# The dt columns of a Mamba projection moved from place 16 to place 2 and computed token-major, and the first half of three layer norms normalised one step earlier

## The chip, the cores and the metric

The kernel runs on one NeuronCore of a Trainium2 chip, as a single program. The metric is the device time of one execution in microseconds (us); lower is better. The core's engines are TensorE (PE in the profile; PEld are its weight loads), VectorE (DVE), ScalarE (ACT), GpSimd (POOL) and the queue that issues most loads (SP). Each runs its own instruction list in order and waits for the others on semaphores.

## The reference

Two transformer blocks run one after the other on 256 tokens of width 1024, in float32. The first block has two layers: attention and an MLP, then a bidirectional Mamba-2 mixer and an MLP, each sublayer followed by a layer norm. The second block (two layers of SwiGLU, convolution with differential attention, SwiGLU) is not touched by the change. What the change touches is this:

```python
def layer_norm(x, g, b):
    xf = x.astype(jnp.float32)
    mu = jnp.mean(xf, -1, keepdims=True)
    var = jnp.mean(jnp.square(xf - mu), -1, keepdims=True)
    return ((xf - mu) * lax.rsqrt(var + LN_EPS)).astype(x.dtype) * g + b

def mamba2_bidir_mixer(x, w_in, conv_w, conv_b, dt_bias, a_log, ...):
    zxbcdt = x @ w_in                      # 256 x 1024 times 1024 x 6208
    z, xbc, dt = jnp.split(zxbcdt, [SSM_D_INNER, SSM_D_INNER + SSM_CONV_DIM], axis=-1)
    xbc = jax.nn.silu(depthwise_conv_centred(xbc, conv_w, conv_b))
    xs, bm, cm = jnp.split(xbc, ...)       # 2048, 1024, 1024 columns
    dt = jax.nn.softplus((dt + dt_bias).astype(jnp.float32))    # 64 columns
    a_neg = -jnp.exp(a_log.astype(jnp.float32))
    # both directions: cumulative sums of dt * a_neg per head, their exponentials,
    # and products with bm, cm and xs in chunks of 128 tokens
    ...
    y = (y_f + y_b) + xs * d_skip[:, None]
    y = y * jax.nn.silu(z)                 # then a grouped RMS norm and the output product
```

## The kernel before

**Weights in units.** Every product with weights is cut into units: 1024 rows by 256 columns of a weight matrix, 1 MB, one after the other through three slots (`RING`). SP loads unit u into `w_raw` once the low part of unit u - 3 is made. ACT rounds it to `w_hi` (`split`, L735; it waits until PE is done with unit u - 3), and DVE or, for units 2 to 16 of the Mamba projection and some later ones, POOL computes the remainder `w_lo` = `w_raw` - `w_hi` (L1132, L646). PE then takes three products of high and low parts, all issued from one line (`three`, L1692). `unit_done` counts the units that PE has finished. In the names of the trace `pg<-op_hi,w_hi` is a product written to the PSUM buffer `pg` in which the activations stream and the weights are stationary; `pg<-w_hi,op_hi` is the other way round.

**Two orientations.** `feature_chunk` (L1699) puts 128 weight columns into the array and streams 256 tokens, so features come out on the partitions. `token_tile` (L1708) puts 128 tokens into the array and streams the weight columns, so tokens come out on the partitions. Both take 8 pieces of the inner dimension by 3 products, 24 matmuls for one result tile. A full unit has two tiles, 48 matmuls.

**The Mamba projection.** It has 25 units in the order of `SSM_COLS`: 16 that go through the convolution (n = 0 to 15: 8 for B and C, 8 for xs), one with the 64 dt columns (n = 16, `DT_AT`), and 8 for z (n = 17 to 24). For a convolution unit DVE does ten operations (L1452, L1456) and ACT a SiLU (`conv_act`, L932) one unit later; the eight xs units are also turned to token-major by PE (L1998) and copied out by DVE (`xs_evac`). The dt unit is one `feature_chunk` of 24 matmuls, after which the 64 dt features lie on 64 partitions (`dt_v`). DVE adds the bias (L1417), ACT computes the parts of softplus (L959 to L962, with an exponential of `a_col` between), DVE joins them two units later (L1420), computes the cumulative sums and the pair `g_pair` (L1425 to L1433), PE turns dt to token-major (L1989) and DVE copies that into `dt_tok` (L1436). All of this is needed only in the stage that follows the projection (chunked scan, from about 505 us).

**The layer norms.** The last unit before a layer norm is ordered so that its four sums of 128 tokens by 512 columns end one after the other (`output` with `last`, L1727). DVE (`ln`, L1175) takes each: it adds the residual (L1183) and takes statistics (L1186); after the second and the fourth sum it combines them for token tile 0 and tile 1 (L1189). ACT computes the standard deviation (L768), DVE its reciprocal (L1173) and the normalised tile `xn` (L1207, one instruction for tile 0, four for tile 1). PE turns `xn` to feature-major (L1757), 8 transposes of tile 0 and 8 of tile 1, in that order; ACT scales each pair of tile 1's (L757), DVE splits it (L1149, L1150), and the next projection begins. In norms 1, 2 and 3 the normalisation of tile 0 stands behind the statistics of the fourth sum; in norm 4, which goes another way, it stands behind the third.

Of the kernel before, what the change touches and what calls it, by code (L numbers as in the profile page):

```python
# [14 lines left out]
P = 128  # L15
# [40 lines left out]
CONV_UNITS = 2 * Z_UNITS  # L56
# [3 lines left out]
XS_AT = 10  # L60
# [136 lines left out]
def two_blocks(nc, A, out):  # L197
    with ExitStack() as ctx:
# [103 lines left out]
        dt_bias = cv(1)  # L302
# [6 lines left out]
        dt_v, dt_a = h32[0:64, 0:T], h32[0:64, T:2 * T]  # L309
# [293 lines left out]
        def _(pool):  # L603
# [68 lines left out]
            pool.dma_start(dt_bias[0:64, :], A["ssm_dt_bias"].rearrange("a (d o) -> (a d) o", o=1)).then_inc(small_in, 16)  # L672
# [9 lines left out]
            pool.wait_ge(g_ready, 1)  # L682
            pool.wait_ge(dtT_done, 1)
# [48 lines left out]
        def _(act):  # L732
# [215 lines left out]

            for n in range(len(SSM_COLS)):
# [3 lines left out]
                if 1 <= n <= CONV_UNITS:  # L953
                    conv_act(n - 1)
                if n > DT_AT:
                    if n == DT_AT + 1:

                        act.wait_ge(dt_sum, 1)
                        link(act.activation(dt_a, dt_v, ACT.Abs))  # L959
                        link(act.activation(dt_a, dt_a, ACT.Exp, scale=-1.0))  # L960
                        act.activation(a_col[0:64, :], a_col[0:64, :], ACT.Exp).then_inc(dt_soft, 1)
                        act.activation(dt_a, dt_a, ACT.Ln, bias=1.0).then_inc(dt_soft, 1)  # L962
                    z = n - DT_AT - 1
                    act.wait_ge(unit_done, u + 1)
                    act.activation(silz[:, :, z * U:z * U + U], pair, ACT.Silu).then_inc(z_ready, 1)
# [155 lines left out]
        def _(dve):  # L1121
# [53 lines left out]
            def ln(u_last, k, apply):  # L1175
# [235 lines left out]
            dve.memset(one_col, 1.0)  # L1411
            for n in range(len(SSM_COLS)):
                split(U_SSM + n + 2)
                if n == DT_AT:
                    dve.wait_ge(unit_done, U_SSM + n + 1)
                    dve.wait_ge(small_in, 64)
                    dve.tensor_scalar(dt_v, pg[0:64, n % 4, 0:T], dt_bias[0:64, :], None, ALU.add).then_inc(dt_sum, 1)  # L1417
                if n == DT_AT + 2:
                    dve.wait_ge(dt_soft, 2)
                    dve.scalar_tensor_tensor(out=dt_v, in0=dt_v, scalar=0.0, in1=dt_a, op0=ALU.max,  # L1420
                                             op1=ALU.add).then_inc(dt_ready, 1)
                if n == DT_AT + 3:

                    dve.wait_ge(dt_ready, 1)
                    link(dve.tensor_scalar(aT[0:64, :], dt_v, a_col[0:64, :], -1.0, ALU.mult, ALU.mult))  # L1425
# [11 lines left out]
                if n < CONV_UNITS:  # L1437
                    i = n
# [22 lines left out]
                if XS_AT <= n < XS_AT + Z_UNITS:  # L1461
                    xs_evac(dve, n - XS_AT)
# [220 lines left out]
        def _(pe):  # L1683
# [285 lines left out]

            for n in range(len(SSM_COLS)):  # L1970
                u = U_SSM + n
                bank = pg[:, n % 4, :]
                if n >= 4:
                    m = n - 4
                    if m < CONV_UNITS:
                        pe.wait_ge(conv_done, m + 1)
                    elif m == DT_AT:
                        pe.wait_ge(dt_sum, 1)
                    else:
                        pe.wait_ge(z_ready, m - DT_AT)  # L1980
# [5 lines left out]
                if n == DT_AT + 3:  # L1986
# [4 lines left out]
                if XS_AT <= n < XS_AT + Z_UNITS:  # L1991
                    j = n - XS_AT
# [201 lines left out]
```

## Time and profile before

| what | value |
|---|---|
| median of 3 runs | 1882.2 us (1876.39 to 1884.85) |
| the profiled execution's own time | 1882.2 us |
| its span in the trace | 1880.3 us |
| mean granted TensorE clock | 0.979 of full speed |
| busy share of the span, PE | 96% |
| DVE, ACT, POOL | 57%, 46%, 15% |
| the chain that ended last: PE, DVE, ACT, issue | 87%, 8%, 3%, 1% |
| projection of the Mamba mixer | 357.9 to 504.9 us |
| layer norms 1, 2, 3 | from about 156, 348 and 625 us |

The span runs from the first to the last instruction of the trace; the execution's own time is 1.9 us longer. Busy shares are averages over very different stages, so each stage is read by itself. PE's matmuls are pipelined: a record lasts about 0.28 us while the next one starts 0.12 us later, so the distance between starts is what a matmul costs, not the length of its record.

### The profile page before, as it was taken

To read this page: it belongs to the slowest core of one execution; us is meant where nothing else is said; L and a number is where in the kernel's file an instruction comes from. 1 tells how busy PE (TensorE), PEld (TensorE's weight loads), DVE (VectorE), ACT (ScalarE), POOL (GpSimd) and SP (SyncE) were. 2 spreads that over 40 slices of the span, in tenths; PEclk is the share of its full clock that TensorE was granted. 3 is DMA by queue.
4 is the path that set the end of the run, shared out by engine and by line. 5 is a ranking of instruction groups with operands and counts; after the bars stand their busy time and mean duration, and the time that the engine had idled before them with its cause. 6 is when DMAs were issued, how large, how long until landed. Compare 5 with 4: busy or idle time off the path is not lost.

```text
span 1880.3 us, 29790 instructions
## 1 busy us (share of the span) xinstructions
PE 1806.5 (96%) x12217; PEld 1655.4 (88%) x12217; DVE 1072.9 (57%) x1438; ACT 863.9 (46%) x1137; POOL 286.1 (15%) x155
## 2 busy tenths in 40 slices
PE   8988999999999899989999998999999999989999
PEld 7757999899997799979998977999899989779998
DVE  5567555668576755564544574454554445745444
ACT  4354444445555344454335646434543446464342
POOL 2003000286241300000000730000000006300000
PEclk9899999999999999989999999999999999989999
DMA  9303655564502465535554521655455554316552
GB/s 298 113 1 129 210 193 184 151 189 143 200 1 89 145 225 190 190 123 187 182 182 153 174 96 59 208 180 184 151 201 180 185 171 158 112 45 202 179 185 105
DMA packets 211135, 293.99 MB, mean 156 GB/s; under 512 B 6426, under 2 KB 184064, under 8 KB 211056
## 3 DMA queue, kind: packets, MB, share of 16 engines
q1 hardware_dynamic: 207936, 285.62, 45.5%
q0 software_dynamic: 2688, 6.47, 1.4%
q8 instruction: 56, 0.92, 0.2%
q10 hardware_dynamic: 432, 0.79, 0.1%
q14 instruction: 23, 0.19, 0.0%
HBM read 291.81 MB, written 1.05 MB: 156 GB/s over the span
## 4 chain that ended last, share of the span: by engine, by line
PE 87%; DVE 8%; ACT 3%; issue 1%; DMA 0%; POOL 0%; SPq 0%; ACTq 0%; DVEq 0%
PE pg L1692 52%; PE acc L1692 26%; PE acc L2037 1%; DVE acc L1566 1%; PE pg L2133 1%; PE pg L1757 1%; PE acc L1958 1%; DVE w_lo L1132 1%; PE pg L1756 1%; PE pg L2021 1%; PE pg L2023 1%; DVE stats L1186 1%; PE pg L1934 1%; DVE X L1183 1%; DVE arena L1627 1%
## 5 line engine op out<-in xcount | busy, mean ns | idle before, releaser
L1132 DVE TENSOR_TENSOR w_lo<-w_raw,w_hi 128x2048 fp32r<-128x2048 f32 x231 | 539.1, 2336 | 393.6 <-ACT w_hi L742 393.5
L1692 PE MATMUL pg<-op_hi,w_hi 128*128 128x256 f32 x2544 | 725.6, 285 | 5.0 <-DVE op_lo L1150 3.1
L1692 PE MATMUL pg<-op_lo,w_hi 128*128 128x256 f32 x2544 | 720.4, 283 | 0.0
L1692 PE MATMUL pg<-op_hi,w_lo 128*128 128x256 f32 x2544 | 720.4, 283 | 0.0
L742 ACT CAST w_hi<-w_raw 128x2048 fp32r<-128x2048 f32 x270 | 514.4, 1905 | 219.3 <-PE pg L1692 141.2
L1692 PEld LDWEIGHTS pg<-op_hi,w_hi 128*128 128x128 f32 x2544 | 488.4, 192 | 13.4 <-issue 7.6
L1692 PEld LDWEIGHTS pg<-op_hi,w_lo 128*128 128x128 f32 x2544 | 488.6, 192 | 3.3 <-issue 0.5
L1692 PEld LDWEIGHTS pg<-op_lo,w_hi 128*128 128x128 f32 x2544 | 488.5, 192 | 0.0
L1692 PE MATMUL acc<-w_hi,op_hi 128*128 128x512 f32 x768 | 303.7, 395 | 5.6 <-DVE op_lo L1256 4.4
L1692 PE MATMUL acc<-w_lo,op_hi 128*128 128x512 f32 x768 | 302.1, 393 | 0.0
L1692 PE MATMUL acc<-w_hi,op_lo 128*128 128x512 f32 x768 | 301.0, 392 | 0.0
L646 POOL TENSOR_TENSOR w_lo<-w_raw,w_hi 128x2048 fp32r<-128x2048 f32 x39 | 179.7, 4611 | 572.1 <-DVE w_lo L1132 435.9
L1692 PEld LDWEIGHTS acc<-w_hi,op_hi 128*128 128x128 f32 x768 | 146.1, 190 | 35.5 <-issue 5.5
L1692 PEld LDWEIGHTS acc<-w_hi,op_lo 128*128 128x128 f32 x768 | 145.7, 190 | 31.3
L1692 PEld LDWEIGHTS acc<-w_lo,op_hi 128*128 128x128 f32 x768 | 146.3, 190 | 27.6
L802 ACT CAST op_hi<-h 128x512 fp32r<-128x512 f32 x76 | 47.1, 620 | 259.4 <-PE acc L1692 213.5
L795 ACT ACTIVATE act_buf<-pg 128x512 f32<-128x512 f32 x76 | 45.4, 597 | 236.6 <-PE pg L1692 236.6
L1256 DVE TENSOR_TENSOR op_lo<-h,op_hi 128x512 fp32r<-128x512 f32 x76 | 55.4, 729 | 113.5 <-ACT op_hi L802 113.5
L1566 DVE SCALAR_TENSOR_TENSOR acc<-arena,pcol,acc 128x256 f32<-128x256 f32 x174 | 71.1, 481 | 0.6
L1692 PE MATMUL pg<-w_hi,op_hi 128*128 128x256 f32 (+1 forms) x240 | 68.6, 286 | 0.0
L1692 PE MATMUL pg<-w_lo,op_hi 128*128 128x256 f32 (+1 forms) x240 | 67.7, 282 | 0.0
L1692 PE MATMUL pg<-w_hi,op_lo 128*128 128x256 f32 (+1 forms) x240 | 67.7, 282 | 0.0
(269 smaller groups left out, 1542.4 us busy)
## 6 DMA issues: line engine op xcount, KB each, us to landing
w_raw<-in_mlp_w SPq DMA_DIRECT2D x64, 1024.0 KB, 5.3
w_raw<-in_ffn_w_gate SPq DMA_DIRECT2D x44, 1024.0 KB, 5.1
w_raw<-in_ffn_w_up SPq DMA_DIRECT2D x44, 1024.0 KB, 5.1
w_raw<-in_ffn_w_down SPq DMA_DIRECT2D x44, 1024.0 KB, 4.8
w_raw<-in_ssm_w_in SPq DMA_DIRECT2D x24, 1024.0 KB, 5.4
w_raw<-in_w_in SPq DMA_DIRECT2D x20, 1024.0 KB, 5.0
w_raw<-in_attn_w_in SPq DMA_DIRECT2D x9, 1024.0 KB, 9.4
w_raw<-in_ssm_w_out SPq DMA_DIRECT2D x8, 1024.0 KB, 4.8
```

The costliest lines, as they stand in the source:

```text
L646: pool.tensor_tensor(w_lo[:, r, :], w_raw[:, r, :], w_hi[:, r, :].bitcast(F32), ALU.subtract) \
L742: act.copy(w_hi[:, u % RING, :], w_raw[:, u % RING, :]).then_inc(hi_ready, 1)
L795: act.activation(act_buf[:, :], src, func).then_inc(act_done, 1)
L802: act.copy(op_hi[:, at_chunk:at_chunk + 2, :], h32[:, :].rearrange("p (c t) -> p c t", c=2)).then_inc(h_hi, 1)
L1132: dve.tensor_tensor(w_lo[:, s, :], w_raw[:, s, :], w_hi[:, s, :].bitcast(F32), ALU.subtract) \
L1183: dve.scalar_tensor_tensor(out=x, in0=x, scalar=ALPHA, in1=acc[:, q, :], op0=ALU.mult, op1=ALU.add).then_inc(x_new, 1)
L1186: ins = dve.bn_stats(stats[:, t, a, :], x)
L1256: dve.tensor_tensor(op_lo[:, dst, :], h32[:, :].rearrange("p (c t) -> p c t", c=2), op_hi[:, dst, :].bitcast(F32), ALU.subtract).then_inc( ...
L1566: ins = dve.scalar_tensor_tensor(out=conv_bank(c) if k < CK - 1 else cacc[:, c, :], in0=uu[:, c, k:k + T], scalar=w, in1=conv_bank(c), op0 ...
L1627: dve.tensor_scalar(n2[:, s, :], m2[:, s, :], -1.0, None, ALU.mult).then_inc(mx2_ready, 1)
L1692: ins = pe.matmul(psum, l, r, start=first and i == 0, stop=last and i == 2)
L1756: return pe.matmul(o, X[:, t, j * P:(j + 1) * P], diag[:, t, :], start=True, stop=True)
```

## The change

It has two parts, which don't depend on each other.

1. The dt unit moves from n = 16 to n = 2, and the rest keep their order: convolution units at n = 0, 1 and 3 to 16, z units at n = 17 to 24. It is computed with `token_tile`, two tiles of 24 matmuls with 64 streamed columns each, in place of one `feature_chunk` with 256 streamed tokens. Tokens lie on the partitions, so the bias is loaded as a row for all 128 partitions, the softplus runs on 128 x 128 elements in place of 64 x 256 and writes `dt_tok` directly, and PE turns `dt_tok` to feature-major for the cumulative sums. On ACT the exponential of `a_col` stands behind the logarithm. DVE waits for the softplus right after it has added the bias, in front of the convolution of n = 3.
2. In norms 1 to 3 tile 0 is normalised after the third sum, before the fourth is added.

```diff
-SSM_COLS = [2 * DI + i * U for i in range(8)] + [DI + i * U for i in range(Z_UNITS)] + [2 * DI + 2 * SG * SN] \
-    + [i * U for i in range(Z_UNITS)]
-DT_AT = CONV_UNITS
+SSM_COLS = [2 * DI + i * U for i in range(2)] + [2 * DI + 2 * SG * SN] + [2 * DI + i * U for i in range(2, 8)] \
+    + [DI + i * U for i in range(Z_UNITS)] + [i * U for i in range(Z_UNITS)]
+DT_AT = 2
...
         # ACT, the projection's loop
+                if n == DT_AT:
+                    act.wait_ge(dt_sum, 1)
+                    link(act.activation(dt_a, dt_v, ACT.Abs))
+                    link(act.activation(dt_a, dt_a, ACT.Exp, scale=-1.0))
+                    act.activation(dt_a, dt_a, ACT.Ln, bias=1.0).then_inc(dt_soft, 1)
+                    act.activation(a_col[0:64, :], a_col[0:64, :], ACT.Exp).then_inc(dt_soft, 1)
+                    continue
...
         # DVE, ln()
-                    if q == 2 and k == 4:
+                    if q == 2:
                         apply(k, 0)
                 if k == 4:
                     rms(5, 0)
-                else:
-                    apply(k, 0)
                 apply(k, 1)
...
         # DVE, the projection's loop
                 if n == DT_AT:
                     dve.wait_ge(unit_done, U_SSM + n + 1)
                     dve.wait_ge(small_in, 64)
-                    dve.tensor_scalar(dt_v, pg[0:64, n % 4, 0:T], dt_bias[0:64, :], None, ALU.add).then_inc(dt_sum, 1)
+                    dve.tensor_tensor(dt_v, pg[:, n % 4, 0:128].rearrange("p (t n) -> p t n", t=TT),
+                                      dt_bias.unsqueeze(1).broadcast_to([P, TT, 64]), ALU.add).then_inc(dt_sum, 1)
+                    dve.wait_ge(dt_soft, 2)
+                    dve.scalar_tensor_tensor(out=dt_tok, in0=dt_v, scalar=0.0, in1=dt_a, op0=ALU.max,
+                                             op1=ALU.add).then_inc(dt_ready, 1)
+                    continue
                 if n == DT_AT + 2:
+                    dve.wait_ge(dtT_done, 1)
+                    link(dve.tensor_scalar(aT[0:64, :], acc[0:64, 0, 0:T], a_col[0:64, :], -1.0, ALU.mult, ALU.mult))
...
-                if n == DT_AT + 4:
-                    dve.wait_ge(dtT_done, 1)
-                    link(dve.tensor_copy(dt_tok, acc[:, 0, 0:P].rearrange("p (t n) -> p t n", t=TT)))
...
         # PE, the projection's loop
                 if n == DT_AT:
                     take(u)
-                    feature_chunk(u, bank[:, 0:T], 0, step=64).then_inc(unit_done, 1)
-                else:
-                    project(u, bank, tokens=n > DT_AT, fresh="ln2_0" if n == 0 else None)
-                if n == DT_AT + 3:
+                    for t in range(TT):
+                        ins = token_tile(u, bank[:, t * 64:t * 64 + 64], t, 0, 64, step=64)
+                    ins.then_inc(unit_done, 1)
+                    continue
+                project(u, bank, tokens=n >= 17, fresh="ln2_0" if n == 0 else None)
+                if n == DT_AT + 1:
                     pe.wait_ge(dt_ready, 1)
                     for t in range(TT):
-                        ins = pe.transpose(acc[:, 0, t * 64:t * 64 + 64], dt_v[:, t * P:t * P + P], ident[0:64, 0:64])
+                        ins = pe.transpose(acc[0:64, 0, t * P:t * P + P], dt_tok[:, t, :], ident[:, :])
                     ins.then_inc(dtT_done, 1)
```

The counts in the semaphore waits, the loops' indices and the turning of the xs units follow the new order.

ACT around the dt unit before, where it stands between the convolution units and z (`h` is the buffer of `dt_v` and `dt_a`; `arena` here is `a_col`, the sums of the convolution or z):

```order
L742 CAST w_hi<-w_raw 128x2048 [waits unit_done,raw_ready1]
L959 ACTIVATE h<-h 64x256 [waits dt_sum]
L960 ACT_TABLE_LOAD
L960 ACTIVATE h<-h 64x256 [waits act_link]
L961 ACTIVATE arena<-arena 64x1 [waits act_link]
L962 ACT_TABLE_LOAD
L962 ACTIVATE h<-h 64x256
L965 ACT_TABLE_LOAD
L965 ACTIVATE arena<-pg 128x2x256 [waits unit_done]
```

And now, behind the split of unit 4 (the row with `unit_done,raw_ready1`):

```order
L739 CAST w_hi<-w_raw 128x2048 [waits unit_done,raw_ready1]
L953 ACTIVATE h<-h 128x128 [waits dt_sum]
L954 ACT_TABLE_LOAD
L954 ACTIVATE h<-h 128x128 [waits act_link]
L955 ACT_TABLE_LOAD
L955 ACTIVATE h<-h 128x128 [waits act_link]
L956 ACT_TABLE_LOAD
L956 ACTIVATE arena<-arena 64x1
L739 CAST w_hi<-w_raw 128x2048 [waits unit_done,raw_ready2]
L942 ACT_TABLE_LOAD
L942 ACTIVATE arena<-arena,pcol 128x256 [waits conv_done]
```

The softplus now stands between the splits of units 4 and 5, with a table load of its own for each of Exp, Ln, Exp and the SiLU that follows, and the splits of all later units stand behind it.

DVE in the second layer norm before, from the third sum on:

```order
L1183 SCALAR_TENSOR_TENSOR X<-X,acc 128x512
L1186 BN_STATS stats<-X 128x6
L1183 SCALAR_TENSOR_TENSOR X<-X,acc 128x512
L1186 BN_STATS stats<-X 128x6
L1189 BN_AGGR mv<-stats 128x2
L1173 RECIPROCAL rstd<-std 128x1
L1207 TENSOR_SCALAR xn<-X,mv,rstd 128x1024
L1173 RECIPROCAL rstd<-std 128x1
L1207 TENSOR_SCALAR xn<-X,mv,rstd 128x256 x4
```

And now:

```order
L1187 SCALAR_TENSOR_TENSOR X<-X,acc 128x512
L1190 BN_STATS stats<-X 128x6
L1177 RECIPROCAL rstd<-std 128x1
L1209 TENSOR_SCALAR xn<-X,mv,rstd 128x1024
L1187 SCALAR_TENSOR_TENSOR X<-X,acc 128x512
L1190 BN_STATS stats<-X 128x6
L1193 BN_AGGR mv<-stats 128x2
L1177 RECIPROCAL rstd<-std 128x1
L1209 TENSOR_SCALAR xn<-X,mv,rstd 128x256 x4
```

The reciprocal and the normalisation of tile 0 moved ahead of the fourth sum; between the combination of tile 1's statistics (BN_AGGR) and the reciprocal that needs ACT's answer to it, nothing is left.

DVE at the dt unit now (`arena<-h` writes `dt_tok`; the rows before and behind are convolutions):

```order
L1456 SCALAR_TENSOR_TENSOR arena<-pg,pcol,arena 128x254 [waits dve_link] x2
L1420 TENSOR_TENSOR h<-pg,arena 128x128 [waits small_in,unit_done]
L1423 SCALAR_TENSOR_TENSOR arena<-h 128x128 [waits dt_soft]
L1452 TENSOR_SCALAR arena<-pg,pcol 128x256 [waits conv_silu,unit_done]
L1452 TENSOR_SCALAR arena<-pg,pcol 128x256
L1456 SCALAR_TENSOR_TENSOR arena<-pg,pcol,arena 128x254 [waits dve_link] x2
```

The add and the joining of the softplus stand next to each other, ahead of the convolution of n = 3; in the kernel before, two splits and two copies stood between them.

## Rows read from the trace of the kernel before

**Rows 1.** The page's fourth part: the chain that ended last, by engine.

```profile
PE 87%; DVE 8%; ACT 3%; issue 1%; DMA 0%; POOL 0%; SPq 0%; ACTq 0%; DVEq 0%
```

**Rows 2.** DVE by time, second layer norm: start us, us, engine, line, operation.

```profile
353.06 0.21 DVE L1189 BATCH_NORM_AGGREGATE mv<-stats 128x2 f32<-128x12 f32 x1
353.18 0.11 DVE L1173 RECIPROCAL rstd<-std 128x1 f32<-128x1 f32 x1
353.33 0.81 DVE L1207 TENSOR_SCALAR xn<-X,mv,rstd 128x1024 f32<-128x1024 f32 x1
354.06 0.15 DVE L1173 RECIPROCAL rstd<-std 128x1 f32<-128x1 f32 x1
354.25 1.38 DVE L1207 TENSOR_SCALAR xn<-X,mv,rstd 128x256 f32<-128x256 f32 x4
```

**Rows 3.** ACT by time, second norm; in brackets idle us before, and the releaser.

```profile
353.30 0.29 ACT L768 ACTIVATE std<-mv,lnb 128x1 f32<-128x1 f32 x1 [2.48 <-DVE mv L1189]
...
355.55 1.93 ACT L757 ACTIVATE turn_buf<-pg,pcol 128x256 f32<-128x256 f32 x4 [1.16 <-PE pg L1757]
```

**Rows 4.** PE by time, second norm: the 16 transposes.

```profile
354.20 1.97 PE L1757 MATMUL pg<-ident,xn 128*128 128x128 f32 x16 [2.77 <-DVE xn L1207]
```

**Rows 5.** ACT, then DVE, by time, fourth norm: a reciprocal released by ACT.

```profile
831.70 0.29 ACT L789 ACTIVATE std<-ssum,part 128x1 f32<-128x1 f32 x1
...
832.03 0.16 DVE L1173 RECIPROCAL rstd<-std 128x1 f32<-128x1 f32 x1 [1.53 <-ACT std L789]
```

**Rows 6.** PE, then ACT, by time, third norm.

```profile
631.98 3.45 PE L1757 MATMUL pg<-ident,xn 128*128 128x128 f32 x16 [2.78 <-DVE xn L1207]
...
634.19 1.93 ACT L757 ACTIVATE turn_buf<-pg,pcol 128x256 f32<-128x256 f32 x4 [2.81 <-PE pg L1757]
```

**Rows 7.** A stretch; the last columns are granted clock, DMA share, GB/s.

```profile
632.00:636.00 4.00, 4.00 (x19) 3.52 (x20) 2.10 (x6) 1.81 (x4) 2.90 (x5) 0.57 0.54 153
```

**Rows 8.** PE by time, dt unit: first and last of 24 matmuls.

```profile
454.48 0.36 PE L1692 MATMUL pg<-op_hi,w_hi 128*128 128x256 f32 x1
...
457.30 0.28 PE L1692 MATMUL pg<-op_lo,w_hi 128*128 128x256 f32 x1
```

**Rows 9.** PE by time, first and last of 48 matmuls with 128 streamed columns.

```profile
26.88 0.22 PE L1692 MATMUL pg<-w_hi,op_hi 128*128 128x128 f32 x1
...
32.07 0.28 PE L1692 MATMUL pg<-w_hi,op_lo 128*128 128x128 f32 x1
```

**Rows 10.** PE by time, scan stage: 8 matmuls with 64 streamed columns.

```profile
523.56 1.00 PE L2037 MATMUL acc<-arena 128*128 128x64 f32 x8
```

**Rows 11.** DVE, then ACT, by time, the dt unit's sum and softplus.

```profile
463.66 0.47 DVE L1417 TENSOR_SCALAR h<-pg,arena 64x256 f32<-64x256 f32 x1
...
464.16 0.42 ACT L959 ACTIVATE h<-h 64x256 f32<-64x256 f32 x1 [2.33 <-DVE h L1417]
464.60 1.28 ACT L960 ACT_TABLE_LOAD   x1
...
466.34 0.20 ACT L961 ACTIVATE arena<-arena 64x1 f32<-64x1 f32 x1
```

**Rows 12.** ACT, POOL, DVE by time, units 1 to 4 of the projection.

```profile
371.64 1.91 ACT L742 CAST w_hi<-w_raw 128x2048 fp32r<-128x2048 f32 x1 [0.75 <-PE pg L1692]
...
373.63 4.63 POOL L646 TENSOR_TENSOR w_lo<-w_raw,w_hi 128x2048 fp32r<-128x2048 f32 x1 [0.94 <-ACT w_hi L742]
...
371.58 0.88 DVE L1452 TENSOR_SCALAR arena<-pg,pcol 128x256 f32<-128x256 f32 x2 [1.64 <-PE pg L1692]
...
377.34 0.88 DVE L1452 TENSOR_SCALAR arena<-pg,pcol 128x256 f32<-128x256 f32 x2 [1.63 <-PE pg L1692]
```

**Rows 13.** DVE, then ACT, by time, units 17 to 20 of the projection.

```profile
459.61 4.13 DVE L1132 TENSOR_TENSOR w_lo<-w_raw,w_hi 128x2048 fp32r<-128x2048 f32 x1
...
475.74 0.60 ACT L965 ACTIVATE arena<-pg 128x512 f32<-128x512 f32 x1 [1.47 <-PE pg L1692]
...
481.94 0.60 ACT L965 ACTIVATE arena<-pg 128x512 f32<-128x512 f32 x1 [3.81 <-PE pg L1692]
```

More of the change, by code:

```diff
@@ L301, in two_blocks @@
         ssm_c = prow[:, :, :].rearrange("p a n -> p (a n)")[:, 0:384]
-        dt_bias = cv(1)
+        dt_bias = cv(64)
         d_skip = cv(SH)
@@ L308, in two_blocks @@
         aT, gT = act_buf[:, 0:T], act_buf[:, T:2 * T]
-        dt_v, dt_a = h32[0:64, 0:T], h32[0:64, T:2 * T]
+        dt_v, dt_a = (h32[:, i * P:i * P + P].rearrange("p (t n) -> p t n", t=TT) for i in range(2))
         xD = [b[:, :].rearrange("p (t n) -> p t n", t=TT) for b in (act_buf, h32)]
@@ L671, in _ @@
             pool.wait_ge(h_ready, HG_MLP[0] + G1)
-            pool.dma_start(dt_bias[0:64, :], A["ssm_dt_bias"].rearrange("a (d o) -> (a d) o", o=1)).then_inc(small_in, 16)
+            pool.dma_start(dt_bias, A["ssm_dt_bias"].broadcast_to([P, 64])).then_inc(small_in, 16)
             pool.dma_start(d_skip, A["ssm_D"].broadcast_to([P, SH])).then_inc(small_in, 16)
@@ L680, in _ @@
             rows_load(2)
-            pool.wait_ge(g_ready, 1)
-            pool.wait_ge(dtT_done, 1)
+            pool.wait_ge(dt_ready, 1)
             pool.wait_ge(small_in, 64)
@@ L947, in conv_act @@
                 ins.then_inc(conv_silu, 1)
+            i = 0
             for n in range(len(SSM_COLS)):
@@ L951, in _ @@
                 split(u + 2)
-                pair = pg[:, n % 4, :].rearrange("p (c t) -> p c t", c=2)
[L953 to L963, printed above, removed]
+                if n == DT_AT:
[5 more added lines that the diff above has]
+                    continue
+                pair = pg[:, n % 4, :].rearrange("p (c t) -> p c t", c=2)
+                if n < len(SSM_COLS) - Z_UNITS:
+                    if i >= 1:
+                        conv_act(i - 1)
+                    i += 1
+                else:
+                    if i == 16:
+                        conv_act(15)
+                        i += 1
+                    z = n - (len(SSM_COLS) - Z_UNITS)
                     act.wait_ge(unit_done, u + 1)
@@ L1411, in _ @@
             dve.memset(one_col, 1.0)
+            i = 0
             for n in range(len(SSM_COLS)):
@@ L1460, in _ @@
                     ins.then_inc(conv_done, 1)
-                if XS_AT <= n < XS_AT + Z_UNITS:
-                    xs_evac(dve, n - XS_AT)
+                    i += 1
+                    if i >= 11:
+                        xs_evac(dve, i - 11)
+                elif i == 16:
+                    xs_evac(dve, 6)
+                    xs_evac(dve, 7)
+                    i += 1
             dve.wait_ge(const_in, CONST_SSM)
@@ L1967, in _ @@
             turn("ln2_0", xn)
+            i = 0
             for n in range(len(SSM_COLS)):
@@ L1974, in _ @@
                     m = n - 4
-                    if m < CONV_UNITS:
+                    if m < DT_AT:
                         pe.wait_ge(conv_done, m + 1)
@@ L1978, in _ @@
                         pe.wait_ge(dt_sum, 1)
+                    elif m < 17:
+                        pe.wait_ge(conv_done, m)
                     else:
-                        pe.wait_ge(z_ready, m - DT_AT)
+                        pe.wait_ge(z_ready, m - 16)
                 if n == DT_AT:
                     take(u)
-                    feature_chunk(u, bank[:, 0:T], 0, step=64).then_inc(unit_done, 1)
-                else:
-                    project(u, bank, tokens=n > DT_AT, fresh="ln2_0" if n == 0 else None)
-                if n == DT_AT + 3:
+                    for t in range(TT):
[4 more added lines that the diff above has]
+                if n == DT_AT + 1:
                     pe.wait_ge(dt_ready, 1)
                     for t in range(TT):
-                        ins = pe.transpose(acc[:, 0, t * 64:t * 64 + 64], dt_v[:, t * P:t * P + P], ident[0:64, 0:64])
+                        ins = pe.transpose(acc[0:64, 0, t * P:t * P + P], dt_tok[:, t, :], ident[:, :])
                     ins.then_inc(dtT_done, 1)
-                if XS_AT <= n < XS_AT + Z_UNITS:
-                    j = n - XS_AT
+                if n >= 11 and n < 19:
+                    j = n - 11
                     pe.wait_ge(conv_silu, j + 9)
```

10 lines of the change are left out of this document (1 added, 9 removed).

## The prediction

> **What bounds the kernel now.** I read the chain that ended last first, then PE's waits, then the engines by time in the two stretches that the change touches. The chain is 87% PE [rows 1], so what changes PE's matmul time or makes PE wait changes the total, and what DVE, ACT and POOL do beside it is free as long as it is early enough. In the projection PE starts a unit every 5.76 us, the distance between two units' convolutions [rows 12], and is never idle. In a layer norm the roles turn: PE stands, and DVE works without a gap from the first sum to the last normalised quarter, so there DVE sets the end [rows 2]. PE waits 2.77 us for tile 0 and then runs all 16 transposes back to back [rows 4].
>
> **The dt unit on PE.** Before: 24 matmuls from 454.48 to 457.30 plus one step, 24 x 0.12 = 2.9 us [rows 8]. After: 48 matmuls, each with a full load of 128 token columns and only 64 streamed columns. The trace has no fp32r matmul of this width. The nearest from above is the same kind with 128 streamed columns: (32.07 - 26.88) / 47 = 0.110 us from start to start [rows 9], hardly less than the 0.12 of 256 columns, so below 256 columns the streamed width no longer sets the pace. The nearest from below is a plain float32 matmul with 64: eight in 1.00 us, of which the last one's tail is about 0.28, so (1.00 - 0.28) / 7 = 0.103 [rows 10]. That gives 4.9 to 5.3 us; I take 5.3, from the row of the same type. Term: 5.3 - 2.9 = +2.4 us, all on PE's path (bounds +2.0 and +2.4 when pipelined; the third rival has them not pipelined).
>
> A rule speaks for less. The Trainium skill, "TensorE: Matmul & The Clock Gate", section "Back-to-back issue gap", puts 1 to 64 streamed columns at about 25 ns, or 62 ns with the sequencer's decoding. By 62 ns the unit would take 3.0 us and the whole come to 1882.8 us (the sixth rival); but the same page says of real streams that the weight load counts too, and the rows with 64 and 128 columns, 0.103 and 0.110, side with that.
>
> **The softplus at its new place.** I work in the clock of the trace before. Unit 1 ends at 371.58, since DVE starts its convolution there [rows 12]. The dt unit, now unit 2, ends 5.3 later, at 376.9; unit 3 at 376.9 + 5.76 = 382.7. From DVE's add to ACT's first operation it took 464.16 - 463.66 = 0.50 with 256 elements; with 128 I take 0.4, so ACT starts at 377.3. Then Abs, load, Exp, load, Ln, load, Exp of `a_col`. A load is 1.28; an operation on 256 elements 0.42, on one 0.20 [rows 11], so on 128 about 0.3; with 0.03 between them it is 3 x 0.3 + 0.2 + 3 x 1.28 + 0.2 = 5.1 us. ACT is done at 382.4.
> - Queued behind it on DVE is the joining (0.3) and the convolution of n = 3, whose data comes at 382.7: nothing lost. PE waits for `dt_ready` after unit 3, so from 382.7 for at most 0.1.
> - Queued behind it on ACT is the split of unit 5, which was free to start at 376.9. It runs 382.4 to 384.3 (1.91), POOL follows 0.08 later and takes 4.63 [rows 12]: the low part of unit 5 is there at 384.4 + 4.6 = 389.0. PE ends unit 4 at 382.7 + 5.76 and the two transposes of dt, worth (481.94 - 475.74) - 5.76 = 0.44 [rows 13]: 388.9. So PE waits 0.1, and the stall of `dt_ready` is part of it.
> - Then ACT also loads the SiLU table and does one convolution before the split of unit 6 (382.4 + 1.9 + 1.3 + 0.9 + 1.9 = 388.4); POOL takes it up at 389.0 and ends at 393.6, PE wants it at 394.7. POOL needs 4.63 of each 5.76, so the slack comes back by 1.1 us per unit.
>
> Term: +0.2 us. Bounds: 0, if the operations take as on one element; +0.8, if they take as long as with 256 (0.4 more) and POOL is slowed a little by DVE's cumulative sums, which now run beside its splits. The 0.44 of the transposes was paid before as well. The three ACT operations, one load less, the copy into `dt_tok` and the sums that leave the z units free nothing: PE was never idle from unit 17 to the end of the projection. The new bias load on POOL's queue is issued where the old one was, ahead of the second norm. SP's loads keep their order otherwise; a dt unit early is a short load early, and slot 2 is then waited for as before.
>
> **The three layer norms.** DVE does the same work in another order. Reciprocal and normalisation of tile 0 take 354.06 - 353.18 = 0.88 and move ahead of the fourth sum. So tile 0's transposes (8 x 0.11) run while DVE works on the fourth sum and are out of the way. But the combination for tile 1 comes 0.88 later, at 353.94 in the second norm, and ACT's answer is no longer hidden behind tile 0: ACT began 0.24 after the combination's start and took 0.29 [rows 3], and a reciprocal that ACT releases starts 0.04 after it ends [rows 5]: 353.94 + 0.57 = 354.51. The normalisation of tile 1 follows 0.19 later, at 354.70, not at 354.25 [rows 2]. Its first quarter (0.40 long) is there at 355.10 and PE can begin tile 1 at 355.16. Before, PE began tile 1 after eight transposes, at 354.20 + 0.88 = 355.08 [rows 4]. The first pair, which ACT waited for (355.55, [rows 3]), is thus 0.1 us later, and everything behind it in the same rhythm. Term: 3 x 0.1 = +0.3 us. Bounds for one norm: -0.88, if tile 0's transposes were all that counted, and +0.45, if tile 1's delay counted in full.
>
> **The sum.** 2.4 + 0.2 + 0.3 = +2.9 us on the profiled execution's own 1882.2 us (span 1880.3 and 1.9 around it), which equals the median: 1885.1 us, +0.15%. I call "same" what is within 0.5% (9.4 us), about what a measurement of this kernel can tell; the three runs of before alone span 8.5 us.
>
> **The rivals.**
> - Second: the layer norms give. In the third norm the granted clock was 0.57 over 632 to 636 [rows 7], 1.2 and not 2.4 GHz for most of it: the 16 transposes took 3.45 us and not 1.97, and ACT's first pair came 2.21 us after PE's start in place of 1.35 [rows 6], 0.86 later. With tile 0's transposes done beforehand only two stand before that pair, so most of 0.86 comes back if the clock falls again; if PE's shorter idle times keep the clock up, that and some matmul time in the second norm come back too. All three norms at -0.88 and 0.9 more make -3.5; with +2.6 for the projection: 1881.3 us. Against it is the count above, in which DVE's chain and not the transposes ends last.
> - Third, slower: the small matmuls don't overlap. If each cost its record of 0.275 us, the dt unit would take 13.2 us, +10.3, and with the rest +10.8: 1893.0 us. It becomes slower by over 0.5% from 0.24 us per matmul on. Both small-width rows, in which starts are 0.10 to 0.11 apart, speak against it.
> - Fourth, slower in part: ACT's chain is twice as dear. Then the low part of unit 5 and all behind it is late. With the four operations and three loads as in the rows there is 0.1 us of lateness, so every further us on ACT goes straight to PE. One us for each of three loads would make +2.9 more: 1888.0 us. The rows show Exp starting right as the load ends (464.60 + 1.28, and 466.34 after two operations of 0.42), so I see no hidden us.
> - Fifth: a late stall. DVE now works on xs copy 7 after unit 18 and only then on the low part of unit 20. POOL's work on X lies there, beside which a DVE split took 4.13 [rows 13]. From the end of unit 18 and its transposes the copy takes 0.7 and the split 4.1, PE wants it after unit 19's 5.76: 1 us to spare. If both are slowed further, some 1 us more: 1886 us.
> - Sixth: the width counts after all below 128 columns, and a matmul with 64 costs about half of 0.110. Then the dt unit takes 2.6 to 3.0 us, its term is 0, and the whole is 1882.8 us. The scan's 0.103 with the same width [rows 10] is against it, though those matmuls are plain float32.
>
> On the fourth, the Trainium skill, "ScalarE: Activation LUTs", section "What ACT_TABLE_LOAD costs", adds a drain of about 1.38 us to each load's 1.28. By that the three loads ahead of the split of unit 5 would cost 4.1 us more, and all of it would be stall: 1889.2 us. The rows show no such gap between operation, load and operation.
>
> **How the numbers follow.** Chances: first 0.59, second 0.15, third 0.04, fourth 0.10, fifth 0.04, sixth 0.05; 0.03 for what I don't see. Half-speed spells of the clock elsewhere shift with every change of phase and can move any of these by 2 or 3 us. The first case's own range is 1882 to 1888; with the second and the fourth it is 1879 to 1890. Slower by over 0.5% takes the third or a fourth at over three times its estimate: 0.05. Faster by over 0.5% would need more than all that the norms can give: 0.03.
>
> **What would show it.** Right: the 48 small matmuls 0.10 to 0.11 us apart; three table loads between DVE's add and the split of unit 5, and a PE wait below 0.5 us at unit 5; in each norm PE's transposes in two groups with idle time between them, DVE idle about 0.5 us before the reciprocal of tile 1, and the first pair at ACT within 0.2 us of before, counted from the first sum. Wrong: a PE gap of over 1 us in units 4 to 6 or 19 to 21; small matmuls over 0.2 us apart; a first pair at ACT 0.5 us earlier in a norm at full clock.

## The result and the profile after

The changed kernel takes 1890.7 us (median of 6 runs, 1886.4 to 1892.4), the kernel before 1881.6 us in its own 6 (1875.9 to 1884.9): 9.0 us more, a ratio of 1.0052 with a 95% interval of 1.0032 to 1.0073. I had predicted 1885.1 us with a range of 1879 to 1890. The sign and the size of the dt unit were right; the whole came out three times as dear as forecast, and just outside the range.

The profiled execution took 1886.6 us. This is the first line of its page, and the chain that ended last by engine:

```profile
span 1884.5 us, 29836 instructions
...
PE 85%; DVE 10%; ACT 3%; issue 1%; DMA 0%; POOL 0%; SPq 0%; ACTq 0%; DVEq 0%
```

The span is 4.2 us longer than before (1880.3). That is less than the 9.0 us of the medians, and for a reason that has nothing to do with the change. In the attention stage, which is the same in both kernels, the clock fell to 1.2 GHz for a different length in the two profiled executions. The stretch 90 to 100 us before (busy us and, in brackets, instructions of PE, its weight loads, DVE, ACT and POOL, then the granted clock, the DMA share and GB/s):

```profile
90.00:100.00 10.00, 10.00 (x25) 5.27 (x24) 4.38 (x14) 3.60 (x14) 0.00 (x0) 0.51 0.00 0
```

And after:

```profile
90.00:100.00 10.00, 9.30 (x41) 5.33 (x40) 6.67 (x22) 4.88 (x18) 0.00 (x0) 1.00 0.01 2
```

The first sum of norm 1 came at 155.56 us before and at 150.35 after: 5.2 us that belong to no edit. In the profiled executions of the ten experiments below it came at 150 to 152 us in eight and at 155 in two (5 and 10), so both moments are seen with the old and with the new order of units. I therefore compare stages. From the first sum of norm 2 to the scan's first output (DVE) it is 172.9 us before and 183.6 after, +10.7; all other stages together, without the 5.2, make -1.3. The projection itself, from its first to its last matmul, went from 146.8 to 157.3 us. Three things fill these 10.5 us (they add up to 10.4).

**The dt unit on PE, +2.4.** Two of its matmuls:

```profile
365.37 0.28 PE L1697 MATMUL pg<-w_hi,op_lo 128*128 128x64 f32 x1
365.48 0.28 PE L1697 MATMUL pg<-w_hi,op_hi 128*128 128x64 f32 x1
```

They start 0.11 apart, as the row with 128 columns [rows 9] had said: 48 of these against 24 at 0.12 [rows 8].

**A PE wait for a low part, +3.3.** I had allowed 0.1 at unit 5; it came at unit 8, and large. PE:

```profile
402.51 0.28 PE L1697 MATMUL pg<-op_lo,w_hi 128*128 128x256 f32 x1
406.08 0.36 PE L1697 MATMUL pg<-op_hi,w_hi 128*128 128x256 f32 x1 [3.29 <-POOL w_lo L644]
```

It goes back to DVE. DVE from the convolution of n = 3 (L1456) on; L1429 to L1437 are the cumulative sums and `g_pair`, which the change put behind it and ahead of the convolution of n = 4:

```profile
380.38 3.33 DVE L1456 SCALAR_TENSOR_TENSOR arena<-pg,pcol,arena 128x254 f32<-128x254 f32 x8
383.62 0.47 DVE L1429 TENSOR_SCALAR act_buf<-acc,arena 64x256 f32<-64x256 f32 x1
384.12 4.23 DVE L1430 TENSOR_TENSOR_SCAN act_buf<-arena,act_buf 64x256 f32<-64x256 f32 x1
388.39 4.66 DVE L1431 TENSOR_TENSOR act_buf<-act_buf 32x256 f32<-32x256 f32 x1
393.08 0.42 DVE L1433 CAST g_pair<-act_buf 64x512 fp32r<-64x512 f32 x1
...
394.44 0.88 DVE L1452 TENSOR_SCALAR arena<-pg,pcol 128x256 f32<-128x256 f32 x2
```

POOL beside it (low parts of units 5 to 7 back to back, then of 8 and 9), and ACT:

```profile
378.59 14.18 POOL L644 TENSOR_TENSOR w_lo<-w_raw,w_hi 128x2048 fp32r<-128x2048 f32 x3 [6.60 <-ACT w_hi L739]
401.38 9.13 POOL L644 TENSOR_TENSOR w_lo<-w_raw,w_hi 128x2048 fp32r<-128x2048 f32 x2 [8.61 <-ACT w_hi L739]
...
371.65 0.31 ACT L953 ACTIVATE h<-h 128x128 f32<-128x128 f32 x1 [4.27 <-DVE h L1420]
...
376.63 1.89 ACT L739 CAST w_hi<-w_raw 128x2048 fp32r<-128x2048 f32 x1
...
398.60 0.91 ACT L942 ACTIVATE arena<-arena,pcol 128x256 f32<-128x256 f32 x2 [11.09 <-DVE arena L1456]
399.41 1.89 ACT L739 CAST w_hi<-w_raw 128x2048 fp32r<-128x2048 f32 x1
```

The first of POOL's three operations ends at 383.2, the second at 387.8 and the third at 392.8. The scan begins at 384.12 and ends at 388.35, 0.5 us after POOL's second; the next operation begins at 388.39 and ends at 393.05, 0.3 after POOL's third. Once POOL pauses, the rest take 0.42 each. POOL gave way too, but by little: its third operation, which started just before the scan got through, took 5.00 us in place of 4.63. The same two operations in the kernel before, at a place where POOL was idle (472.8 to 480.4):

```profile
477.78 0.68 DVE L1426 TENSOR_TENSOR_SCAN act_buf<-arena,act_buf 64x256 f32<-64x256 f32 x1
478.50 0.42 DVE L1427 TENSOR_TENSOR act_buf<-act_buf 32x256 f32<-32x256 f32 x1
```

So the chain of six took 10.8 us (383.62 to 394.41) instead of 2.9 (477.40 to 480.28), and the next convolution came late, ACT waited 11.09 us for it with the split of unit 8 queued behind it (399.41), POOL got that at 401.38, and PE ran dry at 402.5.

**The clock, +4.7.** At half speed the starts of matmuls are 0.21 apart instead of 0.12. Counting the steps of the projection between 0.19 and 0.23 us gives 25 before and 75 after (some ten in each have another reason, such as the turning of the xs units); at 0.094 each that is 2.4 and 7.1 us. Stretches of the changed kernel: the dt unit, its second half, and the time behind the wait:

```profile
365.00:370.00 5.00, 5.00 (x47) 5.00 (x46) 4.08 (x10) 1.90 (x1) 3.94 (x2) 0.99 0.79 250
370.00:376.00 6.00, 6.00 (x30) 6.00 (x30) 0.29 (x1) 4.27 (x6) 2.00 (x1) 0.50 0.64 201
406.00:412.00 6.00, 5.92 (x37) 5.95 (x38) 4.59 (x12) 3.61 (x5) 6.00 (x2) 0.72 0.62 185
```

In the second the clock is at 1.2 GHz nearly throughout, though PE had been issuing a matmul each 0.11 us since 365.26 without a pause. The rows where it changes:

```profile
369.72 0.28 PE L1697 MATMUL pg<-w_hi,op_lo 128*128 128x64 f32 x1
369.83 0.39 PE L1697 MATMUL pg<-w_hi,op_hi 128*128 128x64 f32 x1
370.03 0.40 PE L1697 MATMUL pg<-w_lo,op_hi 128*128 128x64 f32 x1
```

The last of the three stretches has a fall right behind the wait of 3.3 us. Before, the clock was 1.00 over 365 to 380 and 398 to 412; the only spell of its projection was at the first unit, and the changed kernel has that one too, 1.2 us longer within the projection (0.5 us of the 4.7).

**The norms, next to nothing together.** DVE, ACT and PE in the second norm, in the order of time on each:

```profile
341.02 0.69 DVE L1187 SCALAR_TENSOR_TENSOR X<-X,acc 128x512 f32<-128x512 f32 x1 [0.79 <-PE acc L1697]
...
348.12 0.16 DVE L1177 RECIPROCAL rstd<-std 128x1 f32<-128x1 f32 x1 [0.36 <-ACT std L765]
...
349.27 1.93 ACT L754 ACTIVATE turn_buf<-pg,pcol 128x256 f32<-128x256 f32 x4 [0.40 <-PE pg L1762]
...
346.25 1.10 PE L1762 MATMUL pg<-ident,xn 128*128 128x128 f32 x8 [1.25 <-DVE xn L1209]
348.79 1.76 PE L1762 MATMUL pg<-ident,xn 128*128 128x128 f32 x8 [1.45 <-DVE xn L1209]
```

From the first sum to the first pair at ACT it is 349.27 - 341.02 = 8.25 us; before, 355.55 [rows 3] less 347.45 is 8.10. The transposes stand in two groups, DVE idles 0.36 before tile 1's reciprocal. In the first norm the same distance is 8.50 and was 8.14, in the third 8.29 (rows below) and was 8.95 (634.19 [rows 6] less 625.24).

```profile
629.30 0.69 DVE L1187 SCALAR_TENSOR_TENSOR X<-X,acc 128x512 f32<-128x512 f32 x1 [2.59 <-PE acc L1697]
...
637.59 1.93 ACT L754 ACTIVATE turn_buf<-pg,pcol 128x256 f32<-128x256 f32 x4 [1.22 <-PE pg L1762]
```

The stretch 632 to 640 us of the changed kernel:

```profile
632.00:640.00 8.00, 4.69 (x27) 2.85 (x25) 6.77 (x17) 2.63 (x7) 2.73 (x5) 1.00 0.32 29
```

The third norm gives 0.66 us: before, the clock was at 1.2 GHz while all 16 transposes ran [rows 7]; now it is full. That is +0.36, +0.15 and -0.66.

### The profile page after: what moved, and what is told of

Read it like the earlier page. It is cut to its first block, busy times and chain, and to the rows that moved or that the text cites. A ratio compares the mean times of both kernels' runs of the same rounds, so it can differ in the third digit from the quotient of the medians.

```text
span 1884.5 us, 29836 instructions
## 1 busy us (share of the span) xinstructions
PE 1807.6 (96%) x12241; PEld 1658.7 (88%) x12241; DVE 1082.0 (57%) x1437; ACT 864.0 (46%) x1138; POOL 286.6 (15%) x155
## 4 chain that ended last, share of the span: by engine, by line
PE 85%; DVE 10%; ACT 3%; issue 1%; DMA 0%; POOL 0%; SPq 0%; ACTq 0%; DVEq 0%
PE pg L1697 51%; PE acc L1697 25%; PE acc L2047 1%; DVE acc L1571 1%; PE pg L2143 1%; DVE w_lo L1136 1%; ACT w_hi L739 1%; PE pg L2031 1%; PE pg L2033 1%; DVE stats L1190 1%; DVE X L1187 1%; DVE arena L1632 1%; PE pg L1761 1%; PE pg L1762 0%; PE acc L1963 0%
## 5 line engine op out<-in xcount | busy, mean ns | idle before, releaser
L1697 PE MATMUL pg<-w_hi,op_hi 128*128 128x256 f32 (+2 forms) x256 | 73.2, 286 | 0.0
L1697 PE MATMUL pg<-w_lo,op_hi 128*128 128x256 f32 (+2 forms) x256 | 72.5, 283 | 0.0
L1697 PE MATMUL pg<-w_hi,op_lo 128*128 128x256 f32 (+2 forms) x256 | 72.5, 283 | 0.0
```

What stands on the lines that cost most here:

```text
L1697: ins = pe.matmul(psum, l, r, start=first and i == 0, stop=last and i == 2)
```

## The experiments

All were timed in 5 rounds against the kernel before on the same chip. "Stage" below is the time from the first sum of norm 2 to the scan's first output in the profiled execution: 172.9 before, 183.6 in the changed kernel. The theory was: POOL's long operations hold DVE's sums, which makes the wait; the clock falls with the narrow matmuls and behind the wait; the norms are worth nothing. Rivals: the norms cost it; the softplus on ACT costs it; the width of the matmuls alone costs it.

**1. The norms alone** (kernel before with this part of the change):

```diff
-                    if q == 2 and k == 4:
+                    if q == 2:
...
-                else:
-                    apply(k, 0)
```

> The kernel before with the second part of the change alone: tile 0 normalised after the third sum in norms 1 to 3; the dt unit stays at n = 16. If the norms are worth what the prediction says (+0.1 us each), the ratio is 1.000 (+0.3 us) and the first pair reaches ACT within 0.2 us of before, counted from the first sum. If the norms carry a good part of the +9 us, it is 1.002 or more. If they give something back (the second rival), 0.998.

Measured: 1881.5 us against 1880.8, ratio 0.9995 (0.9981 to 1.0009), stage 173.2. In its trace the first pair comes 0.36 and 0.14 us later in norms 1 and 2 and 0.43 earlier in norm 3. Together the reordered norms neither gain nor lose, and the prediction's second rival, 3.5 us back, is out, though its term for the third norm is there in part.

**2. The dt unit alone** (the changed kernel with the edit of experiment 1 undone).

> The changed kernel with the norms as they were before, so the move of the dt unit alone. Theory: the whole loss is in the projection, which went from 146.8 to 157.3 us in the two traces; expected +8 to +11 us on before (ratio 1.005), a PE wait of about 3 us for POOL's low part, and 1.2 GHz for several us from within the dt unit on. Rival: the norms share in it, then +5 or less.

Measured: 1891.7 us, ratio 1.0060 (1.0041 to 1.0078), stage 183.8. All of the loss is here. PE's wait for POOL was 4.27 us this time. On DVE it was another pair of operations that was held, since POOL's operations ended at other times:

```profile
382.51 0.91 DVE L1432 TENSOR_TENSOR_SCAN act_buf<-arena,act_buf 64x256 f32<-64x256 f32 x1
383.46 4.67 DVE L1433 TENSOR_TENSOR act_buf<-act_buf 32x256 f32<-32x256 f32 x1
388.17 4.72 DVE L1435 CAST g_pair<-act_buf 64x512 fp32r<-64x512 f32 x1
```

The scan escaped with 0.91; the operation behind it and the cast took a whole POOL operation each.

**3. The sums late** (changed kernel; the sums back where POOL makes no low parts, and POOL's next work waits for their end):

```diff
-                if n == DT_AT + 2:
+                if n == DT_AT + 17:
...
+            pool.wait_ge(g_ready, 1)
```

> The changed kernel with the cumulative sums of dt (six DVE operations) moved from n = 4 to n = 19, where POOL has no splits any more; PE turns dt at n = 3 as before. Theory: in the change DVE's sums wait for POOL's splits to end (one took 4.23 us and not 0.68, the next 4.66 and not 0.42), the convolution of unit 4, ACT's split and POOL's come late in turn, and PE waits 3.3 us. With the sums late that wait is gone, and the 1.2 GHz that came 2 us behind it: 4 to 5 us faster than the change, +4 to +5 us on before. Rival: ACT's softplus chain makes the wait, since the split of unit 5 stands behind it; then PE's wait of over 1 us stays, and the gain is under 1.5 us.

Measured: 1884.0 us, ratio 1.0018 (1.0001 to 1.0035), stage 177.6. PE waits for POOL no more, though softplus, table loads and narrow matmuls stay: 6.0 of the stage's 10.7 us, or two thirds of the loss by the ratios, were due to the sums' place. DVE's sums there:

```profile
481.63 0.68 DVE L1431 TENSOR_TENSOR_SCAN act_buf<-arena,act_buf 64x256 f32<-64x256 f32 x1
482.35 0.41 DVE L1432 TENSOR_TENSOR act_buf<-act_buf 32x256 f32<-32x256 f32 x1
```

The clock still falls, now just behind the dt unit (its last matmul starts at 374.96, the next unit at 375.07, and the fall comes at 375.2); the stretch 372 to 380 us:

```profile
372.00:380.00 8.00, 8.00 (x57) 8.00 (x57) 2.37 (x7) 4.32 (x6) 4.54 (x1) 0.79 0.69 205
```

**4. 256 columns in the dt unit** (changed kernel; 192 of each 256 columns are computed for nothing):

```diff
-                        ins = token_tile(u, bank[:, t * 64:t * 64 + 64], t, 0, 64, step=64)
+                        ins = token_tile(u, bank[:, t * U:t * U + U], t, 0, U, step=64)
```

> The changed kernel with 256 in place of 64 streamed columns in the 48 matmuls of the dt unit; 192 of them are computed for nothing and not read. By the spacing alone it is slower than the change: 48 x (0.120 - 0.111) = +0.4 us. Theory: the clock fell to 1.2 GHz because the array was streamed only half as densely in that unit (6.8 us at 1.2 GHz from 4.6 us into it, worth 3.2 us); then with full width the clock stays at 2.4 GHz there and it is 2 to 3 us faster than the change. Rival: the fall of the clock is an accident of phase; then +0.4 us, and it shows 1.2 GHz in that place too, or the change loses it in other runs.

Measured: 1888.5 us, ratio 1.0046 (1.0030 to 1.0063), stage 182.0. Over the dt unit, and around the end of the wait of 4.93 us:

```profile
365.00:380.00 15.00, 14.94 (x126) 14.73 (x125) 8.16 (x21) 10.73 (x12) 8.44 (x3) 1.00 0.60 189
405.00:409.00 4.00, 3.75 (x20) 3.78 (x21) 3.96 (x11) 2.71 (x3) 4.00 (x2) 0.59 0.67 197
```

The matmuls are 0.119 apart instead of 0.111, 0.4 us more for the unit, and the clock stays up. Against the changed kernel it is 1.1 us less by the two ratios, which their intervals don't tell from nothing, and 1.6 by the stage, where 2 to 3 had been expected: what the clock gives back goes in part into the wait, 4.93 us in place of 3.29. (The expectation's "half as densely" is no figure of the rows: they show 64 columns in place of 256 at nearly the same spacing.)

**5. POOL's low parts in four pieces** (changed kernel):

```diff
-                pool.tensor_tensor(w_lo[:, r, :], w_raw[:, r, :], ...).then_inc(lo_ready, 1)
+                for q in range(4):
+                    c = slice(q * 512, q * 512 + 512)
+                    ins = pool.tensor_tensor(w_lo[:, r, c], w_raw[:, r, c], ...)
+                ins.then_inc(lo_ready, 1)
```

> The changed kernel with each of POOL's splits issued as four operations on 512 columns in place of one on 2048, for the first and the second block alike; nothing else moves. Theory: a DVE operation with two SBUF operands waits until the POOL operation that is under way has ended, so its longest delay falls from 4.7 to about 1.2 us each; DVE's cumulative sums then take 5 us or less in place of 10.8, the convolution behind them is in time, PE's wait of 3.3 to 4.9 us at this place is gone, and the kernel is 4 to 6 us faster than the change (+3 to +5 on before). Rival: what DVE waits for is the stretch in which POOL is busy at all, three splits in a row; then cutting changes nothing and the wait stays.

Measured: 1870.9 us, ratio 0.9940 (0.9921 to 0.9960), stage 177.7. The same sums at the same place beside POOL, and POOL:

```profile
388.62 1.23 DVE L1432 TENSOR_TENSOR_SCAN act_buf<-arena,act_buf 64x256 f32<-64x256 f32 x1
389.88 1.34 DVE L1433 TENSOR_TENSOR act_buf<-act_buf 32x256 f32<-32x256 f32 x1
391.26 1.40 DVE L1435 CAST g_pair<-act_buf 64x512 fp32r<-64x512 f32 x1
...
384.25 16.19 POOL L646 TENSOR_TENSOR w_lo<-w_raw,w_hi 128x512 fp32r<-128x512 f32 x12 [5.82 <-ACT w_hi L741]
```

POOL's piece is 16.19 / 12 = 1.35 us on average, and every one of DVE's operations now takes 1.2 to 1.4: they pass one per piece. This is what separates the theory from "POOL slows DVE in proportion": the total of work beside them is the same, only the grain changed. Pieces beside DVE's operations took 1.47 us and more, the others 1.3, so POOL gives way here too. PE's wait fell to 0.4 us. The gain went past what I expected (I had looked at the projection only). Two stages of the second block, which the change doesn't touch, became 3.4 and 6.5 us shorter (134.7 to 131.3, 136.3 to 129.8). PE's waits for DVE there (us in total, times, longest us), first before, then in this experiment:

```profile
PE pg L2124 <- DVE arena L1643: 8.6, 4, 3.8
```

```profile
PE pg L2136 <- DVE arena L1650: 2.8, 4, 0.9
```

**6. The kernel before with POOL's work on X in pieces** (256 columns instead of 1024, both products and sums):

```diff
-                    link(pool.tensor_tensor(X[:, t, :], xn[:, t, :], gain_row[:, :], ALU.mult))
+                    for q in range(4):
+                        c = slice(q * 256, q * 256 + 256)
+                        ins = pool.tensor_tensor(X[:, t, c], xn[:, t, c], gain_row[:, c], ALU.mult)
+                    link(ins)
```

> The kernel before with POOL's work on X behind norms 1 to 3 (gain and bias, four operations on 1024 columns per norm) issued as sixteen on 256 columns. Theory: in the trace of before DVE's first square in the MLP behind norm 1 took 2.88 us and not 0.69, and its low part 2.08; both ended as POOL's operations did, PE waited 2.65 us and its clock fell for some us after. With pieces of about 1.1 us these delays shrink to under 1 us each, in norm 3 (a PE wait of 1.74) as well: 3 to 7 us faster than before. Rival: POOL and DVE take turns word by word, then the whole work of POOL costs DVE the same in pieces: no change.

Measured: 1870.7 us, ratio 0.9935 (0.9917 to 0.9953). So the kernel before had the same trouble elsewhere. Behind norm 1, DVE, then POOL, then PE before:

```profile
175.81 2.88 DVE L1260 TENSOR_TENSOR h<-act_buf 128x512 f32<-128x512 f32 x1
179.38 2.08 DVE L1256 TENSOR_TENSOR op_lo<-h,op_hi 128x512 fp32r<-128x512 f32 x1 [0.68 <-ACT op_hi L802]
...
169.43 8.71 POOL L661 TENSOR_TENSOR X<-xn,gain_row 128x1024 f32<-128x1024 f32 x2 [144.18 <-DVE op_lo L1150]
...
181.60 0.71 PE L1692 MATMUL acc<-w_hi,op_hi 128*128 128x512 f32 x1 [2.65 <-DVE op_lo L1256]
```

And here:

```profile
170.22 1.22 DVE L1265 TENSOR_TENSOR h<-act_buf 128x512 f32<-128x512 f32 x1
172.13 1.17 DVE L1261 TENSOR_TENSOR op_lo<-h,op_hi 128x512 fp32r<-128x512 f32 x1 [0.69 <-ACT op_hi L807]
```

The first of them had waited for the end of POOL's second operation (169.43 + 8.71 = 178.14) and ended 0.55 behind it; now it waits for one piece (1.22 us in place of 2.88). PE's wait of 2.65 is gone, norm 1 to norm 2 went from 191.9 to 187.4 us and norm 3 to norm 4 from 193.0 to 189.0. The 10.1 us by the medians are more than the 3 to 7 expected; these two stages give 8.5 of them.

**7. Experiments 3 and 4 together.**

> The changed kernel with both cures: the cumulative sums at n = 19 and 256 streamed columns in the dt unit (192 computed for nothing). Theory: no PE wait for POOL and no fall of the clock within the dt unit; what is left is 48 x 0.12 - 24 x 0.12 = +2.8 us on before. Rival: the clock's fall there is not due to the narrow matmuls; then it comes in this kernel too, and the time is +4 or more.

Measured: 1880.7 us, ratio 1.0003 (0.9989 to 1.0017), stage 176.4; the clock is full from 365 us on and PE doesn't wait for POOL. The interval reaches to +3.2 us, so the +2.8 of the longer dt unit is neither shown nor excluded by the times; the stage is 3.5 us longer than before. With wait and clock gone, nothing that the times can tell from zero is left of the loss.

**8. Place 2, but feature-major** (24 matmuls as before, softplus on 64 x 256; sums late):

```diff
-                    for t in range(TT):
-                        ins = token_tile(u, bank[:, t * 64:t * 64 + 64], t, 0, 64, step=64)
-                    ins.then_inc(unit_done, 1)
+                    feature_chunk(u, bank[:, 0:T], 0, step=64).then_inc(unit_done, 1)
```

> The changed kernel with the dt unit at n = 2 but feature-major as before (24 matmuls with 256 streamed columns, softplus on 64 x 256), the cumulative sums and the copy to dt_tok at n = 19, and the new norms. Theory: the move to n = 2 by itself is free up to the wait behind ACT's softplus: the unit is 2.4 us shorter on PE, so ACT's chain, which hangs on its end, leaves the split of unit 5 no more room than in the change, and PE waits up to 1 us; in all 0 to +1 us on before (ratio 1.000). Rival: the short unit at n = 2 makes the chain of splits late (ACT 5.4 us, POOL 4.6), PE waits 2 us or more, and it is +2 or more.

Measured: 1883.7 us, ratio 1.0006 (0.9989 to 1.0022). Stage 177.2. The times are where I expected them, but the wait isn't: not up to 1 us but 1.85, nearly the rival's 2, with the granted clock at 0.50 right behind it (382.3 to 385.7 us); the stage is 4.3 us longer than before, which the times don't show in full. The short unit leaves too little time for the softplus, and PE waits at the transposes of dt:

```profile
378.58 0.28 PE L1698 MATMUL pg<-op_lo,w_hi 128*128 128x256 f32 x1
380.71 0.34 PE L1998 MATMUL acc<-ident,h 64*128 64x64 f32 x2 [1.85 <-DVE h L1423]
```

So the 5.3 us of the token-major unit are partly paid back: ACT's chain, 5.0 us long, is hidden behind them and the unit after.

**9 and 10. Both cuts** (experiments 5 and 6) in the kernel before, and in the changed one.

> The kernel before with both cuts: POOL's splits in four pieces and its work on X in four pieces per tile. Theory: the two gains are in different stages (MLPs behind norms 1 and 3; attention stages of the second block) and add up: about 10 us from the second block and 10 to 12 from the MLPs, so 18 to 22 us faster than before, ratio 0.989 to 0.991. Rival: more instructions on POOL make its splits late somewhere, then it stops at 0.993.

> The changed kernel with both cuts. What is left of the change once POOL no longer holds DVE up: theory says 2.4 us of matmuls and 2 to 3 us at 1.2 GHz in the dt unit, so it is 4 to 6 us slower than the kernel before with both cuts (ratio to before 0.992 to 0.994). Rival: the difference is nearer 9 us, then there is a cause that the cuts don't touch.

Measured: 1857.9 us, ratio 0.9890 (0.9871 to 0.9909), stage 173.0, and 1862.9 us, ratio 0.9908 (0.9890 to 0.9927), stage 178.1. The first is the best version of all. With DVE's holding out of the way the change costs 5.0 us by medians and 5.1 by the stage. The dt unit is 2.4 of it, 51 steps at half speed against 24, counted as above, are 2.5, and the wait for POOL is 0.2: together 5.1.

## Why the prediction was wrong

- **What bounds the kernel** held: 85% of the chain is PE, and each loss arrived as a PE wait or a slower PE.
- **The dt unit, +2.4**: the spacing was right (0.111 against 0.110), and the sixth and third rivals are out. But the term had only the spacing at full clock. The clock fell 4.6 to 5.4 us after the first matmul of the dt unit in all five kernels with 64 streamed columns: inside the unit in three (the changed one, experiments 2 and 5), within 0.3 us of its end in two (3 and 10). It fell in neither of the two with 256 (4, 7). I had a row of a fall in a norm [rows 7] and used it for a gain only; for the projection I wrote that spells "can move any of these by 2 or 3 us" and left it out of the sum. It belonged in it, at 1.5 to 3 us: the spell was 3.4 us long in four of the five (about 16 matmuls at 0.094) and 6.8 in the changed kernel.
- **The softplus**: ACT's chain was right, 5.0 us measured (371.65 to 376.63) for 5.1, with each operation 0.01 to 0.02 us behind the end of its table load; the fourth rival is out. PE didn't wait for `dt_ready`.
- **The failed step** is the bound of this term: "+0.8, if they take as long as with 256 (0.4 more) and POOL is slowed a little by DVE's cumulative sums". It is mainly the other way round: POOL lost 0.4 us to DVE's sums, but it held DVE. DVE's chain became 10.8 us instead of 2.9, and PE waited 3.3 us (4.3 and 4.9 in experiments 2 and 4), with a fall of the clock behind. A row for it was in my hands: the DVE split of 4.13 beside POOL's work [rows 13], which I used in the fifth rival as a length and not as a rule. I asked what the moved sums would cost POOL, not what POOL, whose low parts run without a pause exactly there, would cost them; at their old place, 477 to 480 us, POOL was idle. Nor would the signs that I named for being wrong have caught it: the wait came at unit 8, not in units 4 to 6 or 19 to 21.
- The Trainium skill says this outright, "SBUF — State Buffer", section "Who interferes with whom": a DVE instruction with two SBUF inputs contends with a GpSimd instruction that reads SBUF, and the one that comes second is blocked until the first is finished. The traces agree with it (4.66 us in place of 0.42 for an operation on 32 x 256 elements), and the convolutions, which read PSUM and one SBUF operand, kept their 0.42 each beside the same POOL operations. I had not weighed this rule.
- **The norms, +0.3**: right for the three together within what can be measured (experiment 1), but not norm by norm: +0.36, +0.15 and -0.66 where 0.1 stood for each. The second rival's term for the clock in the third norm was sound; its 0.88 for every norm did not come. The fifth rival's late stall did not come either.

In sum, for the stage: +2.4 as predicted, +3.3 for the wait where 0.2 stood, +4.7 for the clock where nothing stood. By experiments, from the ratios to the kernel before: taking the sums away from POOL gives back 6.4 us (the wait and the clock's fall behind it), widening the unit alone 1.1, both together 9.2; by the stage it is 6.0, 1.6 and 7.2.

Open: why the clock falls with narrow matmuls issued without a pause was not settled; only that it does, and that the width decides it here. Nor is it known how often the attention stage's spell is the short or the long one; it moved a profiled execution by 5 us here, and the interval of a ratio is 3 to 4 us to either side, so the split of the loss rests on the stages of the traces more than on the times.

## What to carry to other kernels

When an edit moves DVE operations, look up what POOL does at the new place: an operation of DVE that reads two SBUF operands, or a cast between SBUF buffers, waits there until POOL's running one ends, so its price is the length of POOL's operation and not its own. Where the two must run side by side, cut POOL's operations: it cost time on POOL (16.19 / 3 = 5.4 us for a unit in experiment 5, 14.18 / 3 = 4.7 in the changed kernel) and made the kernel before 1.1% faster (experiment 9, both cuts), more than the change lost. And give narrow matmuls a term for the clock, or stream more columns than are needed, which cost 0.4 us on PE here and kept the clock; by itself it gained little, since the wait behind it grew.

## What the runs showed of the hardware that I had not expected

- DVE's hold by POOL has the grain of whole POOL operations, and it takes casts from SBUF to SBUF too: `g_pair` took 4.72 us instead of 0.42 in experiment 2, and 1.40 with POOL's pieces of 1.35.
- PE with matmuls back to back, each 0.11 us, lost the 2.4 GHz clock when they streamed 64 columns (granted clock 0.50 over 370 to 376 us) and kept it with 256 (1.00 over 365 to 380 us) at nearly the same spacing. The Trainium skill, "TensorE: Matmul & The Clock Gate", section "Part 1: The HAM clock gate (the "warmup" mystery)", ties the clock to how busy PE has been; a PE without gaps in its records was not enough for that here.
